# Sum of experts by feature halves, with the following norm's sums and first weights in its program

## The reference

```python
x = x + g1 * m
h = rms_norm(x, norm_g[layer, 1]) * (1.0 + sc2) + sh2
x = x + g2 * peer_ffn(h, ...)
# next layer:  h = rms_norm(x, norm_g[1, 0]) * (1.0 + sc1) + sh1;  u = h @ s5_w_in
# after the last layer:
return rms_norm(x, final_norm_g)

def rms_norm(x, g):
    return x * rsqrt(mean(x * x, axis=-1) + EPS) * g
```

## Time and profile before

| | us |
|---|---|
| median of 3 runs | 3218.54 |
| lowest, highest | 3215.37, 3218.54 |
| the profiled execution | 3217.91 |
| its span | 3216.1 |

### The profile page before, as it was taken

The page is one execution under the profiler, slowest core; times in us unless marked ns, Lnnn a source line. Parts: engine busy times, 40 slices in busy tenths (PEclk is TensorE's granted clock), DMA queues, the critical chain, the costliest instruction groups (busy, mean ns, idle before and its releaser), DMA issues. The chain is left out here.

```text
span 3216.1 us, 48665 instructions
## 1 busy us (share of the span) xinstructions
PE 2968.4 (92%) x17528; PEld 2670.5 (83%) x17528; DVE 2030.7 (63%) x3988; ACT 1256.4 (39%) x1826; POOL 155.5 (5%) x116
## 2 busy tenths in 40 slices
PE   7967797899999999999898888978999999999997
PEld 4946697789999999988687787977899999999885
DVE  8867679953348888878735645899534433443454
ACT  3343344753333333333342234458433333333333
POOL 0000350000000000000000012500000000000000
PEclk9988899999999999999988988999999999999999
DMA  5712233574457767767613232336644444444463
GB/s 207 275 39 102 85 118 122 220 246 155 154 183 246 240 237 236 248 193 229 203 46 121 78 119 79 118 125 236 235 153 145 151 155 153 144 152 155 138 176 109
DMA packets 324479, 524.86 MB, mean 163 GB/s; under 512 B 215536, under 2 KB 218352, under 8 KB 319872
## 3 DMA queue, kind: packets, MB, share of 16 engines
q1 hardware_dynamic: 321472, 472.89, 45.4%
q10 hardware_dynamic: 2880, 50.33, 3.9%
HBM read 449.00 MB, written 74.15 MB: 163 GB/s over the span
## 5 line engine op out<-in xcount | busy, mean ns | idle before, releaser
L1952 PE MATMUL pe_s<-peer_hi,pq_uh 128*128 128x384 f32 x2304 | 784.8, 341 | 23.4 <-DVE peer_lo L163 12.6
L163 DVE TENSOR_TENSOR val_vl<-val_vr,val_vh 128x1024 fp32r<-128x1024 f32 x256 | 313.7, 1225 | 757.8 <-ACT val_vh L2115 757.8
L1954 PE MATMUL pe_s<-peer_hi,pq_ul 128*128 128x384 f32 x2304 | 775.9, 337 | 0.0
L1953 PE MATMUL pe_s<-peer_lo,pq_uh 128*128 128x384 f32 x2304 | 775.7, 337 | 0.0
L2052 ACT ACTIVATE pe_A<-pe_s 128x384 f32 (+1 forms) x256 | 126.1, 493 | 1127.2 <-PE pe_s L1954 1127.2
L2019 PE MATMUL peer_acc<-val_vh,val_wh 128*128 128x512 f32 x1536 | 473.2, 389 | 1.0 <-DVE val_wl L163 1.0
L2019 PE MATMUL peer_acc<-val_vh,val_wl 128*128 128x512 f32 x1536 | 474.1, 390 | 0.0
L2019 PE MATMUL peer_acc<-val_vl,val_wh 128*128 128x512 f32 x1536 | 472.9, 389 | 0.0
L1952 PEld LDWEIGHTS pe_s<-peer_hi,pq_uh 128*128 128x128 f32 x2304 | 436.4, 189 | 43.5 <-issue 17.2
L1953 PEld LDWEIGHTS pe_s<-peer_lo,pq_uh 128*128 128x128 f32 x2304 | 436.9, 190 | 8.4
L1954 PEld LDWEIGHTS pe_s<-peer_hi,pq_ul 128*128 128x128 f32 x2304 | 436.4, 189 | 0.0
(11 more groups left out here) (458 smaller groups left out, 3519.6 us busy)
## 6 DMA issues: line engine op xcount, KB each, us to landing
pq_ur<-in_peer_u SPq DMA_DIRECT2D x256, 512.0 KB, 3.7
val_vr<-in_peer_v SPq DMA_DIRECT2D x256, 512.0 KB, 4.5
val_gr<-gates SPq DMA_DIRECT2D x256, 192.0 KB, 4.6
val_mrow<-in_ada_rows SPq DMA_DIRECT2D x56, 512.0 KB, 4.3
gates<-gate_stg ACTq DMA_DIRECT2D x6, 4096.0 KB, 12.5
pq_ur<-in_w_query SPq DMA_DIRECT2D x32, 512.0 KB, 3.6
s_wv<-val_out SPq DMA_DIRECT2D x32, 512.0 KB, 5.2
gates<-gate_stg ACTq DMA_DIRECT2D x4, 3072.0 KB, 13.0
```

The source lines that it names most:

```text
L163: return nc.vector.tensor_tensor(r32(out), x, hi, ALU.subtract)
L1952: pe.matmul(o, r32(uh[:, b, k]), r32(hi[:, k]), start=k == 0, stop=False)
L1953: pe.matmul(o, r32(uh[:, b, k]), r32(lo[:, k]), start=False, stop=False)
L1954: mm = pe.matmul(o, r32(ul[:, b, k]), r32(hi[:, k]), start=False, stop=k == KC - 1)
```

## The change

`add_experts` now takes what follows into its own program.

- It goes through the banks by feature halves: all three token tiles of features 0 to 511, then those of 512 to 1023.
- After the copies ACT squares x, k = 0 to 3 when three pieces have been added and k = 4 to 7 when six have; PE sums the squares behind its transposes, into the first PSUM bank of `acc`; ACT takes the root and DVE the reciprocal in the same program.
- After layer 0 (`following` is given) SP loads the first two blocks of the S5 input weights at the start of that program, into buffers that `s5_input` uses later for a table (`par.post`). ACT waits for both loads, makes the high part of block 0 and only then squares; DVE makes its low part after its last add and before the reciprocal. `s5_input` then starts with the scalings. `parts(1)` and the clearing of borders come after them on DVE, and block 0 is not split there any more. SP asks for blocks 2 and 3 at once, ahead of the tables.
- After layer 1 (`following` is None) DVE multiplies x by gain and reciprocal in one scalar_tensor_tensor for each k, and SP stores each k (192 KB) when it is ready. `norm` with its block is gone.
- `Norm.shifts` and `Norm.scales` are cut in two (`roots`, `invert`), so that `mix_experts` runs what it ran.

The core of the diff:

```diff
+class Following:
+    def __init__(self, nc, sems, d):
+        self.nc, self.d = nc, d
+        with Stage(nc, sems, "fs") as s:
+            s.sb("below", [P, 2 * KC * T + KC + 2 * P + S5Tables.KEPT + KC * 2 * QP * SLOTS])
+            self.raw = s.sb("raw", [P, 2, KC, P])
+            self.hi, self.lo = s.sb("hi", [P, KC, P]), s.sb("lo", [P, KC, P])
+            self.root, self.rstd = s.sb("root", [P, T]), s.sb("rstd", [P, T])
...
+        order = [(half, t) for half in range(2) for t in range(NT)]
...
+            @block.sync
+            def _(sp):
+                if following is not None:
+                    for b in range(2):
+                        sp.dma_start(following.raw[:, b], d["s5_w_in"][b]).then_inc(loaded, 16)
+                    sp.wait_ge(loaded, 32)
+                else:
+                    for k in range(KC):
+                        sp.wait_ge(normed, k + 1)
+                        sp.dma_start(d["y"][:, k], h[:, k]).then_inc(stored, 16)
+                    sp.wait_ge(stored, 16 * KC)
...
+                for half, t in order:
+                    nc.scalar.activation(out[:, t, half * 512:(half + 1) * 512], acc[:, 2 * t + half, :], ACT.Copy).then_inc(copied, 1)
+                if following is not None:
+                    act.wait_ge(loaded, 32)
+                    nc.scalar.activation(r32(following.hi[:]), following.raw[:, 0], ACT.Copy).then_inc(high, 1)
+                for k in range(KC):
+                    act.wait_ge(added, NT * (k // 4 + 1))
+                    nc.scalar.activation(sq[:, k], cx.x[:, k], ACT.Square).then_inc(squared, 1)
+                act.wait_ge(summed, 1)
+                nc.scalar.activation(root[:], ss, ACT.Sqrt, bias=cx.eps[:, 0:1], scale=1.0 / D).then_inc(rooted, 1)
...
+                for k in range(KC):
+                    pe.wait_ge(squared, k + 1)
+                    mm = pe.matmul(ss, cx.ones[:], sq[:, k], start=k == 0, stop=k == KC - 1)
+                mm.then_inc(summed, 1)
...
+                if following is not None:
+                    dve.wait_ge(high, 1)
+                    lo_part(nc, following.lo[:], following.raw[:, 0], following.hi[:])
+                dve.wait_ge(rooted, 1)
+                nc.vector.reciprocal(rstd[:], root[:]).then_inc(inverted, 1)
+                if following is None:
+                    dve.wait_ge(inverted, 1)
+                    for k in range(KC):
+                        nc.vector.scalar_tensor_tensor(h[:, k], cx.x[:, k], cx.finalg[:, k:k + 1], rstd[:], ALU.mult, ALU.mult).then_inc(normed, 1)
...
-                for i in range(NW):
-                    sp.dma_start(w[:, i], d["s5_w_in"][i]).then_inc(loaded[i], 16)
+                for i in range(NW, 2 * NW):
+                    sp.dma_start(w[:, i % NW], d["s5_w_in"][i]).then_inc(loaded[i % NW], 16)
...
-                nm.sums(pe, ss[:])
...
-                nm.squares(act)
-                nm.shifts(act, ss[:])
+                nm.shifts(act)
...
-                for i in range(NW):
-                    parts(i)
+                nm.scales(dve)
+                parts(1)
                 for c in (0, CP + 1, SLOTS):
                     v.memset(par.uc[:, :, c:c + 1], 0.0)
-                for dr, a, b, c in ((0, 0, CP + 1, SLOTS - 1), (1, CP, SLOTS - 1, CP + 1)):
+                for dr, a, b in ((0, 0, CP + 1), (1, CP, SLOTS - 1)):
                     for e in (a, b):
                         v.memset(quads4(par.pre[:].rearrange("p q r g n -> p (q r) g n"), dr)[:, :, :, e:e + 1], 0.0)
+                parts(2)
+                for dr, c in ((0, SLOTS - 1), (1, CP + 1)):
                     v.memset(quads4(par.post[:].rearrange("p q r g n -> p (q r) g n"), dr)[:, :, :, c:c + 1], 0.0)
-                nm.scales(dve)
-                parts(2)
```

More of the change, by code:

```diff
@@ L520, in inner @@
         dve.wait_ge(self.own, self.n)
[L523 to L582, removed]
@@ L593, in __init__, with roots, shifts @@
         self.scaled, self.shifted, self.high, self.ready = (s.sem(f"n_{x}") for x in ("scaled", "shifted", "high", "ready"))
[L595 to L605, removed]
+    def roots(self, act, ss):
+        act.wait_ge(self.summed, 1)
+        self.nc.scalar.activation(self.root, ss, ACT.Sqrt, bias=self.cx.eps[:, 0:1], scale=1.0 / D).then_inc(self.rooted, 1)
+    def shifts(self, act):
         nc, cx = self.nc, self.cx
-        act.wait_ge(self.summed, 1)
-        nc.scalar.activation(self.root, ss, ACT.Sqrt, bias=cx.eps[:, 0:1], scale=1.0 / D).then_inc(self.rooted, 1)
         for k in range(KC):
@@ L2407, in _ @@
             @block.scalar
             def _(act):
-                for n in range(2 * NT):
-                    nc.scalar.activation(out[:, n // 2, (n % 2) * 512:(n % 2 + 1) * 512], acc[:, n, :], ACT.Copy).then_inc(copied, 1)
+                for half, t in order:
[3 more added lines that the diff above has]
+                    nc.scalar.activation(r32(following.hi[:]), following.raw[:, 0], ACT.Copy).then_inc(high, 1)
@@ L2412, in _ @@
+                for k in range(KC):
[3 more added lines that the diff above has]
+                nc.scalar.activation(root[:], ss, ACT.Sqrt, bias=cx.eps[:, 0:1], scale=1.0 / D).then_inc(rooted, 1)
             @block.tensor
             def _(pe):
-                for n in range(2 * NT):
+                for n, (half, t) in enumerate(order):
                     pe.wait_ge(copied, n + 1)
@@ L2490, in _ @@
                 sp.dma_start(par.masks[:], d["s5_masks"]).then_inc(kept, 16)
-                for i in range(NW, KC):
-                    sp.wait_ge(split, i - NW + 1)
+                for i in range(2 * NW, KC):
+                    sp.wait_ge(split, i - NW)
                     sp.dma_start(w[:, i % NW], d["s5_w_in"][i]).then_inc(loaded[i % NW], 16)
@@ L2940, in build @@
         sems.clear()
-        peer(nc, sems, cx, d, 0, ahead)
+        following = Following(nc, sems, d)
+        peer(nc, sems, cx, d, 0, ahead, following)
         sems.clear()
@@ L2956, in build @@
         sems.clear()
-        peer(nc, sems, cx, d, 1, ahead)
-        norm(nc, sems, cx, "fin", None, None, final=d["y"])
+        peer(nc, sems, cx, d, 1, ahead, None)
 def col_tiles(w):
```

65 lines of the change are left out of this document (38 added, 27 removed).

## The result

The changed kernel took 3201.97 us, the median of five runs (3200.01 to 3202.88); the kernel before took 3218.54 in five (3212.77 to 3223.41). The ratio is 0.995, with a 95% interval of 0.9936 to 0.9965.

The account below looks back on a forecast made before the run. PE, busy 92% of the span, was taken as the bound, so savings had to lie where it has nothing to do. The end's -7.6 and the middle's -0.85 gave -8.45 us, from 3217.91 to 3209.5; range 3204.5 to 3216.

Parts of the forecast that it names:

- Where the gain comes from: Only the two places after the long expert programs gain: -7.6 us at the kernel's end, -0.85 between the layers.
- rival D: The clock stays full at both places and returns earlier: end -0.8 more, between the layers -2.6, 3206 us; chance 0.12.
- Start of the sums: PE's sums of squares begin right behind its last transposes: -2.16 us at the end, -3.1 between the layers.
- Length of the sums: PE's 16 matmuls take 6.3 us instead of 7.12 at the end (-0.8), and stay at 8.09 between the layers.
- rival A: Transposes leave PE too idle, so sums at both places take 11 us at the lower clock; 3217.1 us, chance 0.12.
- Scaling: At the end, eight scalar_tensor_tensor instructions on DVE take 4.4 us instead of 6.15: -1.75 us.
- Stores: At the end, eight 192 KB stores overlap, leaving only the last landing, 2.2 us instead of 5.1: -2.9 us.
- Rival B: The end's small stores complete one behind the other at 4.6 us each; about 3240 us, chance 0.06 shared with another loss.
- The moved barrier: Between the layers, the program change now lies between the reciprocal and the first scaling: +1.4 us.
- The lost cover: Between the layers, weight block 1 is split after the norm's pieces, so the second product waits: +0.85 us.
- The range: Whole kernel between 3204.5 us, the best clock case less a microsecond and a half of spread, and 3216.

Follow-up runs that it names:

- end only: The kernel before with only what follows the last layer replaced by the new form; 3205.80 us, ratio 0.9971 to the kernel before.
- middle only: The changed kernel with the old end, so only what follows layer 0 is new; 3212.32 us, ratio 0.999 to the kernel before.
- second set: The unedited changed kernel timed again beside its two halves, against the kernel before at 3216.24 us; 3208.26 us, ratio 0.997.

## Why the prediction was right or wrong

**Where the gain comes from: right.** Two places and nothing else; end only and middle only carry what the whole change does. 7.6 us were forecast for the end. It gave 9.2 in the first pair of traces and 9.7 on average (31.4 in the two traces with the old end, 21.7 in the eight with the new one; those whose edit changes the end itself are left out). For the middle 0.85 were forecast; 4.4 in the first pair, 2.9 on average (41.1 in two, 38.2 in six). Together 12.6, against 8.45. The first trace of the changed kernel was the case of rival D, the clock full at both places, which had a chance of 0.12 and a time of 3206.

**Start of the sums: right, a little short.** -2.16 forecast at the end, -2.39 measured (+8.58 to +6.19 from the first copy); -3.1 between the layers, -3.65 measured there, since the clock stayed up among the transposes too and they ended earlier. Both are bounded by the transposes, as worked out. The load landed 4.8 us after its issue, not 5.1, and was covered (to within 0.15 us in all traces).

**Length of the sums: the step that failed.** The mechanism stood in the text: the fall at 3194.4 followed a break that the change takes away. But only half of it was put into the sum at the end (6.3; measured 5.33 in the first trace, 5.6 on average of nine), and nothing at all between the layers, where the length "is left" at 8.09; measured 5.43, and 5.9 on average of nine. That is 1.0 and 2.7 us in the first trace, 3.7 of the 5.1 us by which the two stretches beat the sum (13.6 against 8.45). The full-rate length itself was read too long: the windows of rows 3 give 3.4 us at the lower level and not 2.95, so 7.12 - 3.4/2 = 5.4 and not 5.64. The rest of the 5.1 are the earlier starts (0.8), the stores (0.3) and the second product (0.3).

The rule of transposes, rival A, gave the sums 8 us or more at either place; no sums right behind the transposes took more than 6.7. The Trainium skill's page "TensorE: Matmul & The Clock Gate", Part 4: PE-mode transpose, says that transposes don't count as PE being busy the way matmuls do. The traces agree in part: in seven of the eighteen cases the clock fell while PE did nothing but transpose, and in eleven it held, with the same work at the same pace.

**Scaling: right.** 4.4 forecast, 4.32 measured, at a mean of 614 ns for one.

**Stores: right in size, short by 0.3.** One piece lands in 1.9 us, not 2.2. From DVE's end to the end of the span it was 5.52 and is 2.33. Rival B, one piece behind the other at 4.6, didn't come: eight issues in 4.04 us, each landing in 1.9, lie on top of each other.

**The moved barrier: right.** 1.49 from the reciprocal's end to the first scaling; 1.4 was forecast. **The lost cover: right.** From the first to the second product it was 11.05 us (1609.01 to 1620.06) and is 11.90: the 0.85 of the text. The kernel with block 1 split ahead has no break there. What the break does to the clock was put at 0, between -1.5 and +1.5; the averages above say +1.0, without showing it.

**The range: too narrow at the low end.** With the measured stretches in place of the forecast ones the sum is 3217.91 - 13.6 = 3204.3, just below the range. The other 2.3 us down to the median are 1.4 that the two profiled executions differ by elsewhere, and 0.9 between the profiled execution and the median. The range allowed a microsecond and a half for spread around the best case for the clock. But the medians of three sets of the same kernel lie 6.3 us apart (3202.0 to 3208.3), and single runs of the kernel before 10.6. This spread is nearly as large as the gain, and the granted clock in stretches that nobody edits goes along with it: the S5 scan alone took 186.8 to 192.8 us in one and the same kernel. The three runs that were shown before lay 3.2 apart and hid this. Of the 16.6 us of the first set the two stretches account for 11 to 13.6. The rest is luck: all five runs of the changed kernel had a high clock (0.967 or 0.968), while the times of the five of the kernel before spread over 10.6 us. The second set's median, 3208.26, lies inside the range, and that is luck of the other sign.

What stays open: why six of seven runs in the second set lie within 1.2 us of each other near 3208 and the seventh at 3201.5, and what decides whether the clock falls among the transposes.

## What to carry to other kernels

Where a short chain of engines follows a long product, put its first step into the program that ends the product, ordered so that a part of the input is complete halfway; what it saves is the start, and on top of it often the clock, because PE doesn't stand still before the next matmuls. Price such a place at both levels of the clock. Where PE's break of 2 us stayed, the sums here took 1.5 to 3.1 us more than at the full rate; where it was gone, they ran at the full rate in eleven cases and took about 1 us more in seven. When a gain of 0.3% is to be measured, read the edited stretches in the traces: their gain lay between 11.1 and 13.6 us in the three traces of the changed kernel, where the medians of its three sets moved by 6.

## What the runs showed of the hardware that was not expected

- Behind a break of PE of 1.9 us or more the sums ran partly at the lower clock in seven of seven cases, in two of which it had fallen ahead of the break; behind one of 0.93 us they did not. The same 16 matmuls took up to 8.4 us instead of 5.3. The fall can come after PE has gone back to work: 1.1 and 1.4 us into the sums behind breaks of 1.90 and 1.98 us.
- The granted clock can fall while PE turns 128x128 blocks with pauses of 0.4 us (seven of twenty places in the changed order, two of six in the old one), and stays up in the others with the same work.
- Products that nobody needs can pay: with them in PE's idle time between the layers, and weight block 1 split ahead, the stretch took 34.0 and 35.3 us, against 37.0 with the split alone and 36.9 to 39.2 with neither, though PE did more.
- The same program differs by 10.6 us from run to run (five runs of the kernel before). In the 27 runs of another set its mean granted clock, from 0.963 to 0.967, went along with the time: 3219.3 to 3213.2 us on average.
